# Column sums of six modulation vectors: blocks of 32x32 and one small matmul in place of eight matmuls with a column of ones

## The reference

```python
cond = silu(c)                                  # 1024 values
mod = cond @ ada_w[i] + ada_b[i]                # 1024 x 6144 matrix, six vectors of 1024
shift1, scale1, gate1, shift2, scale2, gate2 = split(mod, 6)
h = rmsnorm(x, norm1_g[i]) * (1 + scale1) + shift1
x = x + gate1 * attention(h)
h = rmsnorm(x, norm2_g[i]) * (1 + scale2) + shift2
x = x + gate2 * swiglu(h, f_w_in[i], f_w_out[i])
```

## Time and profile before

| | |
|---|---|
| median of 3 runs | 1042.89 us (1042.69 to 1043.04) |
| the profiled execution's own time | 1042.97 us |
| its span in the trace | 1041.2 us |
| mean granted TensorE clock | 0.992 of full speed |
| PE busy | 993.8 us, 95% |
| DVE busy | 729.5 us, 70% |
| ACT busy | 548.5 us, 53% |
| POOL busy | 66.5 us, 6% |
| HBM traffic | 210 GB/s over the span |

### The profile page before, as it was taken

How to read it: one execution, slowest core, us unless ns; L and a number is a source line. 1 busy time by engine, 2 the same in 40 slices (tenths; PEclk the granted TensorE clock), 3 DMA queues, 4 the chain that set the end, 5 groups by cost and what they waited for, 6 DMA issues and landing times.

```text
span 1041.2 us, 12793 instructions
## 1 busy us (share of the span) xinstructions
PE 993.8 (95%) x4744; PEld 814.4 (78%) x4744; DVE 729.5 (70%) x1025; ACT 548.5 (53%) x893; POOL 66.5 (6%) x118
## 2 busy tenths in 40 slices
PE   2999799999999999999999999999999999999997
PEld 2787577888888787777888886888888778888785
DVE  4988888876778797887665446647753777777653
ACT  4456836544443485575444436575546375455441
POOL 2100222000000401010000002000000010000000
PEclk9999999999999999999999999999999999999999
DMA  9998166998889473449865563856444467565551
GB/s 340 357 343 312 43 203 222 357 310 281 285 270 363 171 237 127 133 125 308 266 203 192 181 190 103 270 164 205 128 140 142 127 189 231 172 187 187 162 182 41
DMA packets 126966, 219.86 MB, mean 211 GB/s; under 512 B 9235, under 2 KB 78088, under 8 KB 126904
## 3 DMA queue, kind: packets, MB, share of 16 engines
q1 hardware_dynamic: 125488, 216.05, 63.1%
q0 software_dynamic: 1088, 2.87, 0.9%
q10 hardware_dynamic: 328, 0.12, 0.0%
HBM read 217.96 MB, written 1.05 MB: 210 GB/s over the span
## 4 chain that ended last, share of the span: by engine, by line
PE 82%; DVE 8%; ACT 4%; DMA 2%; issue 2%; POOL 1%; SPq 0%; DVEq 0%; POOLq 0%; ACTq 0%
PE bank L1844 16%; PE bank L1846 16%; PE bank L1845 16%; PE bank L1859 5%; PE bank L1861 5%; PE bank L1860 5%; DVE w_lo L1130 3%; PE bank L1906 2%; PE bank L1908 2%; PE bank L1907 2%; PE bank L1964 1%; ACT w_hi L625 1%; DMA raw<-in_f_w_in 1%; DVE ada_acc L1160 1%; PE bank L1940 1%
## 5 line engine op out<-in xcount | busy, mean ns | idle before, releaser
L1130 DVE TENSOR_TENSOR w_lo<-raw,w_hi 128x1024 fp32r<-128x1024 f32 x312 | 378.1, 1223 | 221.2 <-ACT w_hi L625 220.7
L625 ACT ACTIVATE w_hi<-raw 128x1024 fp32r<-128x1024 f32 x312 | 326.8, 1059 | 333.2 <-PE bank L1846 183.9
L1844 PE MATMUL bank<-w_hi,h_hi 128*128 128x512 f32 x768 | 307.2, 400 | 3.7 <-DVE w_lo L1130 3.7
L1846 PE MATMUL bank<-w_hi,h_lo 128*128 128x512 f32 x768 | 300.5, 391 | 0.0
L1845 PE MATMUL bank<-w_lo,h_hi 128*128 128x512 f32 x768 | 299.8, 390 | 0.0
L1844 PEld LDWEIGHTS bank<-w_hi,h_hi 128*128 128x128 f32 x768 | 144.8, 189 | 34.3 <-issue 6.1
L1846 PEld LDWEIGHTS bank<-w_hi,h_lo 128*128 128x128 f32 x768 | 144.6, 188 | 31.1
L1845 PEld LDWEIGHTS bank<-w_lo,h_hi 128*128 128x128 f32 x768 | 144.9, 189 | 29.5 <-issue 1.0
L1859 PE MATMUL bank<-w_hi,u_hi 128*128 128x512 f32 x200 | 78.6, 393 | 0.8 <-ACT av L1077 0.8
L1861 PE MATMUL bank<-w_hi,u_lo 128*128 128x512 f32 x200 | 77.9, 389 | 0.0
L1860 PE MATMUL bank<-w_lo,u_hi 128*128 128x512 f32 x200 | 77.9, 389 | 0.0
(11 more groups left out here) (313 smaller groups left out, 1255.1 us busy)
## 6 DMA issues: line engine op xcount, KB each, us to landing
raw<-in_f_w_in SPq DMA_DIRECT2D x176, 256.0 KB
ada<-in_ada_w SPq DMA_DIRECT2D x86, 512.0 KB, 5.8
raw<-in_w_in SPq DMA_DIRECT2D x46, 512.0 KB
raw<-in_f_w_out SPq DMA_DIRECT2D x44, 512.0 KB
raw<-in_w_up SPq DMA_DIRECT2D x88, 256.0 KB
raw<-in_a_w_qkv SPq DMA_DIRECT2D x24, 512.0 KB
raw<-in_w_down SPq DMA_DIRECT2D x22, 512.0 KB
raw<-in_b_w_qkv SPq DMA_DIRECT2D x12, 512.0 KB
```

The costliest lines, as they stand in the source:

```text
L625: nc.scalar.activation(w_hi[:, m % SPL], raw[:, m % RAW], ACT.Copy).then_inc(hi_done, 1)
L1130: ve.tensor_tensor(w_lo[:, m % SPL], raw[:, m % RAW], w_hi[:, m % SPL].bitcast(F32), ALU.subtract).then_inc(lo_done, 1)
L1844: mm(o, hi, w_hi[:, s, k], start=(u == 0 and k == 0), stop=False)
L1846: last = mm(o, lo, w_hi[:, s, k], start=False, stop=(u == 3 and k == 1))
```

## The change

Six of the eight vectors that are not gates (3, 4, 6, 7, 9, 10) are summed in another way. Behind the last fold of such a vector, DVE transposes the accumulator in blocks of 32x32, into the tile that was just folded, and sums each run of 32, which gives `block_sums`, 128x32: lane 32a+i, column b holds the sum of the accumulator's lanes 32a to 32a+31 in column 32b+i. Only then is `ada_done` counted up. PE multiplies `block_sums` by a constant matrix `same_lane`, which has a one where two lanes are equal modulo 32: one matmul of 32 columns sums the four lane groups. `take_vector` picks columns by lane group, in four instructions of 32 lanes each. POOL builds `same_lane` once behind its first norm: one memset and seven `affine_select`, each waiting for the one before. DVE's second step also waits until the reduction of the vector before has read `block_sums`.

```diff
+BY_BLOCKS = (3, 4, 6, 7, 9, 10)
...
             norm(0)
+            lanes = same_lane[:].rearrange("p a n -> p (a n)")
+            nc.gpsimd.memset(lanes, 0.0).then_inc(lane_ok, 1)
+            for n, d in enumerate((-3, -2, -1, 0, 1, 2, 3)):
+                pool.wait_ge(lane_ok, n + 1)
+                nc.gpsimd.affine_select(out=lanes, in_=lanes, compare_op=ALU.not_equal, fill=1.0, base=32 * d,
+                                        pattern=[[-1, P]], channel_multiplier=1).then_inc(lane_ok, 1)
...
-                    ve.scalar_tensor_tensor(out=acc, in0=w, scalar=cond[:, k:k + 1], in1=acc, op0=ALU.mult,
-                                            op1=ALU.add).then_inc(ada_done, 1)
+                    last = ve.scalar_tensor_tensor(out=acc, in0=w, scalar=cond[:, k:k + 1], in1=acc, op0=ALU.mult, op1=ALU.add)
+                    if k < 7 or g not in BY_BLOCKS:
+                        last.then_inc(ada_done, 1)
+                    else:
+                        link(last)
+                        link(ve.transpose(w, acc))
+                        v_.wait_ge(ada_red, COLUMN[g])
+                        ve.tensor_reduce(block_sums[:], w.rearrange("p (b r) -> p b r", r=32), AX.X, ALU.add).then_inc(ada_done, 1)
...
             def take_vector(g):
                 v_.wait_ge(ada_red, COLUMN[g] + 1)
+                if g in BY_BLOCKS:
+                    for b in range(4):
+                        lanes = slice(32 * b, 32 * b + 32)
+                        last = ve.tensor_tensor(mod[lanes, 8 * g:8 * g + 8],
+                                                bank[6][lanes, 0:32].rearrange("p (q b) -> p b q", b=4)[:, b],
+                                                vecs[lanes, ADAB_V + 8 * g:ADAB_V + 8 * g + 8], ALU.add)
+                    last.then_inc(ada_col, 1)
+                    return
...
                 pe.wait_ge(ada_done, 8 * (g + 1))
                 if g:
                     pe.wait_ge(ada_col, COLUMN[g])
+                if g in BY_BLOCKS:
+                    pe.wait_ge(lane_ok, 8)
+                    mm(bank[6][:, 0:32], same_lane[:].rearrange("p a n -> p (a n)"), block_sums[:], start=True,
+                       stop=True).then_inc(ada_red, 1)
+                    return
```

More of the change, by code:

```diff
@@ L218, in program @@
         ada_row = at_p("ada_row", [P, D], 9216)
+        same_lane = at_p("same_lane", [P, 4, 32], 10240)
+        block_sums = at_p("block_sums", [P, 32], 10368)
         stage_v = at_p("stage_v", [P, 3, P], 10752)
@@ L254, in program @@
         table_ok = sem("table_ok")
+        lane_ok, blocks_ok = sem("lane_ok"), sem("blocks_ok")
         ada_red = sem("ada_red")
```

## The result

The changed kernel takes 1046.3 us (median of ten runs) against 1043.26 for the kernel before in the same runs: a ratio of 1.0027, with a 95% interval of 1.0019 to 1.0035. It is slower by 0.3%: small, but the interval does not reach 1. The profiled execution took 1047.78 us, the longest of the ten, with a span of 1046.0. So its trace holds 4.86 us against the first trace of before, where the medians hold 3.0.

The account below looks back on a forecast made before the run. PE, busy 95% of the span, was taken as the bound. Terms 2.7 - 2.96 - 0.35 + 1.9 + 0.1 + 1.1 gave +2.5 us on the profiled 1042.97, which stands 0.1 over the median: 1045.4, range 1041.8 to 1049.4.

Parts of the forecast that it names:

- The added work on DVE: Behind a vector's last fold: transposition and reduction make everything behind them on DVE 2.64 us later.
- Vector 3: Ahead of vector 4's folds: earlier pair transposes remove DVE's 0.43 us of idle, -0.4 us; PE's saving is waited away.
- First boundary: At vector 4: DVE's residual and PE's transposes come later with nothing covering it, +2.7 us.
- Vectors 6 and 7: In the first layer's feed-forward: DVE's free time takes up the added work, PE saves 1.48 us each, -2.96.
- Vector 9: Fold only 2.95 us ahead of the reduction: PE waits for `block_sums`, 1.15 of 1.48 us is given back, -0.35.
- Second boundary: At vector 10: DVE's later scaling delays PE's transposes, PE stands about 3 us, +1.9 us.
- Clock: Behind PE's third new gap, at the second boundary: clock falls to 1.2 GHz, +1.1 us, bounds 0 and 1.6.
- The second gap's fall: Clock also falls behind PE's wait at the first boundary's transposes: priced 0, bounds 0 and 1.6; as rival 1047.0, chance 0.08.
- the cheap insertion: Rival: fold, transposition and reduction delay DVE by under 1.4 us in place of 2.64, so faster; chance 0.13.
- the doubled transposition: Rival: DVE's transposition lasts twice as long, +1.22 us at both boundaries, vector 9 loses its saving, 1049.1; chance 0.16.
- the same without a fall of the clock: Rival: same mechanism, but PE's new gaps do not lower the clock, +1.4 us, 1044.3; chance 0.25.
- nothing to be seen: Rival: transfers moved on SP or unseen slack in the boundaries give back the rest, 1043; chance 0.04.

Follow-up runs that it names:

- The take at group 84: Changed kernel with only vectors 6 and 7 summed by blocks, vector 7's take behind tile 84 instead of 81: 1039.22 us against 1042.77 before.
- version with the late reduction: Changed kernel with only vector 9 by blocks, its reduction behind group 104 instead of 93, its take behind 110 instead of 99: 1043.61 us, ratio 1.0004.
- version with twelve fillers: Whole change plus twelve unread float32 matmuls on PE ahead of the second boundary's transposes: 1044.88 us against 1043.21 before, ratio 1.0017.
- the moved low parts in both versions: DVE's two first-boundary low steps put behind the scaling: in the whole change 1045.52 us; with only vectors 6 and 7, take behind 84, 1039.80.

## Why the prediction was right

It said 1045.4, and slower as the likeliest side; 1046.3 came. The mechanism held: PE's saving is kept where PE is never idle, and lost at the two boundaries to DVE's chain and the clock. Step by step:

- **PE, what goes and comes.** 1.48 a vector was forecast, 1.57 measured: the two new records take 0.14 from start to start at full clock (250.14 to the next at 250.28), not 0.22.
- **The added work on DVE.** 2.64 was forecast. From the start of vector 4's folds to the take it is 155.40 - 147.50 = 7.90 in place of 5.36: 2.54. At vector 10 it is 2.52. The Trainium skill (Vector Engine (DVE) Microarchitecture Reference, "The reshape front-end and per-opcode configuration") says that the transpose passes one element per cycle per lane, from which my estimate was 1.2 us; the trace agrees, with 1.25.
- **The four-part take at its step.** 0.5 was forecast. It moves the next start from 0.08 to 0.70, +0.62: four parts at 0.17 to 0.18 each. The Trainium skill's rule (VectorE: DVE Perf Modes, "Two Vector instructions with no wait between them"), by which each part is held until the last has ended, agrees.
- **Vector 3.** -0.4 was forecast, -0.57 measured, mostly by the idle time ahead of the folds that went. PE's saving there was waited away, 0.57 us of it for `att`. SP's moved count cost nothing that shows.
- **First boundary.** 163.2 was forecast for the transposes, 163.58 measured; PE's wait ahead of the reduction was to be over 4 us and was 3.90, since PE came 0.56 earlier (152.27 against 152.83) and not up to 1.5. The residual came as forecast (+2.59 for +2.7). The step that was mis-sized is `take_vector(4)`, left out of the sum behind the residual: its extra 0.5 passes to the second wait, because it delays DVE's two `w_lo`, and POOL's L547 ends when these do.
- **Vectors 6 and 7.** -2.96 was forecast, -3.13 measured, and 0.65 given back at vector 7's take, which the forecast did not price at all: it looked at when the reduction's input is ready, not at what stands behind the take on DVE. The take at group 84 gives it back.
- **Vector 9.** -0.35 was forecast, +0.08 measured. PE waits 0.76 for `block_sums` where 1.15 was forecast. But what stands behind it on DVE was priced at 0, "where PE is awaited anyway": the insertion uses up those waits of DVE, and PE then waits 0.66 for `xn` at 358.61. The version with the late reduction shows the same.
- **Second boundary.** +1.9 was forecast and +1.81 measured, with the wait of about 3 us (2.97). `take_vector(10)` hides under POOL's root as forecast: DVE's idle time ahead of the scaling falls from 1.58 to 1.05.
- **Clock.** +1.1 was forecast behind this wait. The trace has +2.08, beyond the bound of 1.6, since the clock stays at 1.2 GHz for nearly 6 us and not 3.1; the version with twelve fillers puts it at 1 to 1.4 in the median, and one trace with the same wait has no fall. The second gap's fall, priced at 0, is not there as such: at the first boundary the clock is at 0.50 from 158 to 160 us, behind the first gap and ahead of the transposes. It makes PE 1.6 us later there (offset 0.87 at its first matmul behind the reduction, 2.45 at the last ahead of the transposes), and the wait for the transposes takes that up, as the slack of 2 us in the forecast said.
- **POOL.** 0.1 was forecast. Its build took 6.8 us (15.29 to 22.10), not 4, its seven `affine_select` 6.46 of that, each 0.29 to 1.25 us beside DVE, and costs nothing by the version that has the build alone. The 0.1 in the sum stood on no row.

By the terms the sum is +3.28 - 3.13 + 0.65 + 0.08 + 1.81 and 1 to 1.4 for the clock: +3.7 to +4.1, where the medians show +3.0. The missing 1 us is about what a fall of the clock in the first boundary costs the kernel before and not the changed one (0.84 to 0.91, above), but was not pinned down. That the number came within 0.9 us is in part luck: the terms as measured add up to 1.2 to 1.6 us more than the forecast's +2.5.

Of the rivals, the cheap insertion is refuted by 2.54 us on DVE, the doubled transposition by 1.25, and the same without a fall of the clock by the windows of the profiled execution, though it can be right for a part of the executions. The clock's fall behind the second gap did not come, and nothing to be seen is refuted by the interval.

## What to carry to other kernels

Price work that moves from a saturated engine to a less busy one place by place: here the same edit gains 1.57 us where PE is never idle and loses about 2 to 3 where DVE's chain releases PE, and only the first kind should be kept. An instruction split into parts costs at its own place and at every place where something awaited stands behind it; move it behind that, which cost one number and gave the 0.65 us back in the trace. A gap in PE costs its length and then, in a part of the executions, the clock; filler whose result nobody reads gave 1 to 1.4 us of that back in the median. And where PE waits for DVE, an instruction added to DVE is not free because DVE is idle: ask whom DVE is waiting for, and who comes earlier after the change.

## What was not expected of the hardware

- A one-column instruction of POOL takes 0.30 us alone and up to 2.31 when it meets DVE's `w_lo`, ending with them; moving these brought 0.31. The Trainium skill (SBUF — State Buffer, "SBUF: two separate sides") has the rule, a lock that a DVE instruction with two inputs in the SBUF holds against one of POOL that reads it; these rows agree, and the prediction had not looked for it.
- The clock falls in places where nothing was changed, and in some executions only. Behind 109 us it fell in eight of the fourteen traces, both of before among them, and not in the other six (vectors 3 and 4 alone, the moved low parts in both versions, vector 9 with the late reduction, the fillers at the second boundary, the build alone); each of these six gains about 1.5 us against before from 110 to 114 us. By 32 us the offsets spread from -0.3 to +2.2 us. Such amounts are as large as most terms of this change, and with one trace for a kernel they must be taken out before a boundary is compared.
